# Two transformer-like blocks on one core: state matrices made earlier, the states' products in two portions, and another beginning of the program

## The reference

```python
# first stack, for layer in (0, 1)
h = h + token_mixer(rmsnorm(h), ...)     # a product with w_in gives v, q, k, u, gates; pooling; dilated attention
h = h + conv_ffn(rmsnorm(h), ...)        # a product of width 2 x 2816, a convolution over 3 tokens, gelu, gate, a product back
x = rmsnorm(h)
# second stack, layer 0: gated recurrence (hgrn2) beside a state-space layer (s5)
abar = exp(a * dt)                                 # complex, 32 groups x 64 states
s_t  = abar * s_{t-1} + bb @ u_t                   # "states"
y    = re(c @ s_t) + d * u_t ; z = gelu(y) ; z * sigmoid(z @ w_glu + b_glu)
h = h + concat(hgrn2, s5) @ w_out ; h = h + conv_ffn(...)
# layer 1: latent attention, conv_ffn, and a last rmsnorm
```

## Time and profile before

| | |
|---|---|
| median of 3 runs | 1554.23 us |
| the profiled execution | 1555.74 us |
| its span, first to last instruction | 1554.0 us |
| PE busy | 1497.6 us (96%) |
| DVE / ACT / POOL busy | 1098.1 / 769.0 / 471.2 us |
| mean clock granted to TensorE | 0.986 |

### The profile page before, as it was taken

One profiled execution on the slowest core, in us unless ns is written; L12 is line 12 of the kernel. 1 busy time (PEld: TensorE's weight loads), 2 busy tenths in 40 slices (PEclk: granted clock), 3 DMA queues, 4 the chain that ended last, 5 costly groups with the idle time before them and its releaser, 6 DMA issues.

```text
span 1554.0 us, 24766 instructions
## 1 busy us (share of the span) xinstructions
PE 1497.6 (96%) x10640; PEld 1364.8 (88%) x10640; DVE 1098.1 (71%) x1169; ACT 769.0 (49%) x869; POOL 471.2 (30%) x288
## 2 busy tenths in 40 slices
PE   6999999999999979999999999999999998899997
PEld 4899999888888978999888879898888898888886
DVE  6657666788767537666888555957987568688863
ACT  5433454666444323545656346346665444566542
POOL 1205300244209758001354813001444000135510
PEclk9999999999999989999999998899999999999999
DMA  6574344555554653366455443334554534355552
GB/s 248 196 217 173 134 180 175 188 190 190 176 198 174 252 205 121 136 247 228 183 190 183 152 157 133 110 109 163 190 190 177 186 131 138 109 170 186 188 189 81
DMA packets 48009, 269.72 MB, mean 174 GB/s; under 512 B 11259, under 2 KB 14587, under 8 KB 18716
## 3 DMA queue, kind: packets, MB, share of 16 engines
q1 hardware_dynamic: 47900, 268.13, 48.6%
HBM read 261.30 MB, written 6.82 MB: 173 GB/s over the span
## 4 chain that ended last, share of the span: by engine, by line
PE 85%; POOL 6%; DVE 4%; DMA 2%; ACT 2%; issue 1%; SPq 0%; DVEq 0%; ACTq 0%; POOLq 0%
PE gemm L564 32%; PE gemm L535 29%; PE aux L564 15%; POOL s_made L2041 2%; POOL s_cw L2041 2%; DVE w_lo L1361 2%; DMA raw<-in_weights 1%; POOL pool_w L2041 1%; ACT w_hi L1016 1%; PE aux L586 1%; PE gemm L955 1%; PE aux L535 1%; PE aux L760 1%; PE gemm L645 1%; DMA s_bc<-in_s_c 1%
## 5 line engine op out<-in xcount | busy, mean ns | idle before, releaser
L1361 DVE TENSOR_TENSOR w_lo<-raw,w_hi 128x2048 fp32r<-128x2048 f32 (+3 forms) x248 | 568.8, 2295 | 222.7 <-ACT w_hi L1016 219.7
L1016 ACT ACTIVATE w_hi<-raw 128x2048 fp32r<-128x2048 f32 (+3 forms) x248 | 460.7, 1858 | 359.5 <-PE gemm L535 204.7
L535 PE MATMUL gemm<-x_two,w_hi 128*128 128x256 f32 x1952 | 359.0, 286 | 0.0
L535 PEld LDWEIGHTS gemm<-x_two,w_hi 128*128 128x128 f32 x1952 | 307.8, 194 | 0.9 <-issue 0.2
L535 PE MATMUL gemm<-x_two,w_lo 128*128 128x256 f32 x976 | 277.8, 285 | 0.0
L564 PE MATMUL gemm<-x_two,w_hi 128*128 128x512 f32 x672 | 234.7, 399 | 0.0
L2041 POOL TENSOR_TENSOR tmp<-tmp 128x512 f32<-128x512 f32 x24 | 35.5, 1478 | 551.6 <-ACT tmp L1043 551.5
L535 PEld LDWEIGHTS gemm<-x_two,w_lo 128*128 128x128 f32 x976 | 188.9, 194 | 0.0
L564 PE MATMUL gemm<-y_two,w_hi 128*128 128x512 f32 x528 | 185.2, 396 | 0.0
L564 PE MATMUL gemm<-x_two,w_lo 128*128 128x256 f32 x672 | 174.9, 281 | 0.0
L2161 POOL TENSOR_TENSOR cv<-cv,rstd 128x512 f32<-128x512 f32 x44 | 117.0, 2659 | 174.6 <-ACT cv L1095 174.6
(11 more groups left out here) (364 smaller groups left out, 2726.4 us busy)
## 6 DMA issues: line engine op xcount, KB each, us to landing
raw<-in_weights SPq DMA_DIRECT2D x224, 1024.0 KB, 4.8
raw<-in_weights SPq DMA_DIRECT2D x16, 768.0 KB, 4.2
raw<-in_weights SPq DMA_DIRECT2D x4, 576.0 KB, 3.6
s_inputs<-s_made SPq DMA_DIRECT2D x1, 2048.0 KB, 7.3
s_outputs<-s_cw SPq DMA_DIRECT2D x1, 2048.0 KB, 7.3
s_v<-s_inputs SPq DMA_DIRECT2D x1, 2048.0 KB, 10.1
s_cw<-s_outputs SPq DMA_DIRECT2D x1, 2048.0 KB, 9.6
raw<-in_weights SPq DMA_DIRECT2D x4, 512.0 KB, 3.8
```

The source lines that it names most:

```text
L535: mm = pe.matmul(out, lhs, rhs, start=fresh and m == 0, stop=end and m == 2, skip_group_check=True)
L1016: me.give(act.activation(w_hi[i % SPL][:, 0:n], raw[i % RAW][:, 0:n], ACT.Copy), w_hi_ready)
L1361: me.give(v.tensor_tensor(w_lo[i % RAW][:, 0:n], raw[i % RAW][:, 0:n], w_hi[i % SPL][:, 0:n].bitcast(F32), ALU.subtract), w_lo_ready)
```

## The change

It has four parts.

1. **State matrices.** `s5_inputs` on POOL moves from behind layer 1's first norm sum to the gap behind the first network's last gate (before the norm sum). SP stores `s5_made` at v+1 instead of v+11, and `s5_cw` at v+15 instead of v+18. DVE waits for the second store before it writes gates over its source.
2. **Norm of the mixer.** In both mixers the sum of squares stands behind v1 instead of v0 on PE, the columns behind v2; ACT's root and DVE's reciprocal and v1's emptying move one block back with them.
3. **States' products.** `s5_from_states` is cut in two portions, one on each side of a block; ACT's gelu and DVE's low part of the result move behind other work. `s5_within` on DVE goes from one slot (4) to two (6 and 7).
4. **Program start.** x comes in four pieces, block 0 in two, the first 8 parameter columns alone and first; ACT and DVE work in that order; the squares come last of the inputs; ACT starts with a dummy copy; PE starts with 18 dummy products of a 128x128 tile of ones.

```diff
 # SP
-            load(h[:, :, :], a["x"].rearrange("(c p) s -> p c s", p=P), x_in)
-            load(par[:, :], a["params"], par_in)
+            load(par[:, 0:DC], a["params"][:, 0:DC], par0_in)
+            load_x(0)
+            load(raw[0][:, 0:HALF0], w0[:, 0:HALF0], raw0_in)
+            load_x(1)
+            load(raw[0][:, HALF0:WIDE], w0[:, HALF0:WIDE], raw_in[0])
+            load_x(2)
+            load_x(3)
...
-                if i == first("v", 1) + 11:
+                if i == first("v", 1) + 1:
                     sp.wait_ge(v_made, 1)
...
-                if i == first("v", 1) + 18:
+                if i == first("v", 1) + 15:
                     sp.wait_ge(cw_made, 1)
 # PE
+                if i == 0:
+                    parts = [range(0, 2), range(2, 4)]
...
-                    if j == 0:
...
+                    if j == 1:
                         norm(classes=True)
-                    if j == 1:
+                    if j == 2:
...
+            for k in range(WARM):
+                pe.matmul(A[:, 0:P], ones[:, :], ones[:, :], start=True, stop=True)
...
-            s5_from_states()
+            s5_from_states((0, 1))
             gemm(i + 8, x_hi, x_lo)
+            s5_from_states((2, 3))
             chunk_scores()
 # ACT (DVE alike)
+            first_feed(0)
+            act.wait_ge(raw0_in, 16)
+            me.give(act.activation(w_hi[0][:, 0:HALF0], raw[0][:, 0:HALF0], ACT.Copy), w0_hi_half)
+            first_feed(1)
+            act.wait_ge(raw_in[0], 16)
+            me.give(act.activation(w_hi[0][:, HALF0:WIDE], raw[0][:, HALF0:WIDE], ACT.Copy), w_hi_ready)
+            split(1)
+            first_feed(2)
+            first_feed(3)
+            for j in range(4):
+                me.give(act.activation(tmp[:, 2 * j:2 * j + 2, :], h[:, 2 * j:2 * j + 2, :], ACT.Square), pair_squared)
+            split(2)
 # DVE
             def s5_within(k):
-                if k != 4:
+                if k not in (6, 7):
                     return
...
-                for q in range(4):
+                for q in ((0, 1), (2, 3))[k - 6]:
...
+                if layer:
+                    v.wait_ge(cw_out, 16)
 # POOL
                     ffn(0)
+                    me.settle()
+                    s5_inputs()
                     sum_squares()
...
                 if layer:
-                    s5_inputs()
                     s5_outputs()
```

More of the change, by code:

```diff
@@ L38 @@
 SPL = 3
+HALF0 = WIDE // 2
+WARM = 18
 BANK = 512
@@ L432, in weights @@
                      a["weights"][OFFSETS[i] * P:OFFSETS[i + 1] * P].rearrange("(p n) -> p n", p=P), raw_in[i % RAW])
-            for i in range(RAW):
+            for i in range(1, RAW):
                 weights(i)
+                if i == 1:
+                    load(par[:, DC:NPAR], a["params"][:, DC:NPAR], par_in)
             load(relb[0:BUCKETS, :], a["rel_bias"], relb_in)
@@ L770, in s5_from_inputs, with s5_from_states @@
                                   start=g % 2 == 0 and d == 0, stop=False, skip_group_check=True)
-            def s5_from_states():
-                me.take(s_ready)
-                pe.wait_ge(cw_in, 16)
+            def s5_from_states(groups):
+                if 0 in groups:
+                    me.take(s_ready)
+                    pe.wait_ge(cw_in, 16)
                 m = None
-                for g in range(4):
+                for g in groups:
                     for c in range(T5):
@@ L1151, in mixer, with first_feed @@
                 feed_after(first("wo", layer), named(f"norm2.{layer}"))
-            act.wait_ge(par_in, 16)
[L1154 to L1160, removed]
+            me.take(ones_ready)
+            act.activation(small[:, 43:44], small[:, 0:1], ACT.Copy)
+            act.wait_ge(par0_in, 16)
+            def first_feed(j):
+                act.wait_ge(x_in[j], 16)
+                for c in (2 * j, 2 * j + 1):
+                    ins = act.activation(by_place(x_hi[:, c, :]), in_fours(h[:, c, :]), ACT.Copy, scale=vec("norm1.0", c))
+                me.give(ins, x_hi_ready)
+            first_feed(0)
[10 more added lines that the diff above has]
+            split(2)
+            act.wait_ge(par_in, 16)
             dt, mag = ang[3], ang[4]
@@ L1247, in _ @@
             split_next(i + 7)
+            split_next(i + 8)
+            act.wait_ge(h_ready, 1)
+            sigmoid_in(0)
+            me.take(ket_psum)
+            me.give(act.activation(ket.rearrange("p k n -> p (k n)"), A[:, 2 * BANK:4 * BANK], ACT.Copy), ket_ready)
             me.take(ys_ready)
@@ L1604, in _ @@
             me.give(v.memset(small[:, 1:4], 0.0), ones_ready)
-            v.wait_ge(par_in, 16)
[L1606 to L1612, removed]
+            v.wait_ge(par0_in, 16)
+            feed(0, named("norm1.0"), classes=True)
+            v.wait_ge(w0_hi_half, 1)
+            me.give(v.tensor_tensor(w_lo[0][:, 0:HALF0], raw[0][:, 0:HALF0], w_hi[0][:, 0:HALF0].bitcast(F32),
+                                    ALU.subtract), w0_lo_half)
+            feed(1, named("norm1.0"), classes=True)
+            v.wait_ge(w_hi_ready, 1)
+            me.give(v.tensor_tensor(w_lo[0][:, HALF0:WIDE], raw[0][:, HALF0:WIDE], w_hi[0][:, HALF0:WIDE].bitcast(F32),
+                                    ALU.subtract), w_lo_ready)
+            split(1)
+            feed(2, named("norm1.0"), classes=True)
+            feed(3, named("norm1.0"), classes=True)
+            split(2)
+            v.wait_ge(par_in, 16)
             theta, red = ang[5], ang[6]
```

51 lines of the change are left out of this document (31 added, 20 removed).

## The result

| | before | after |
|---|---|---|
| median | 1554.22 us (4 runs, 1549.85 to 1558.14) | 1527.81 us (4 runs, 1527.12 to 1528.96) |
| the profiled execution / its span | 1555.74 / 1554.0 us | 1528.17 / 1526.4 us |
| PE idle in the span | 56.4 us | 31.1 us |

What follows compares the result with a forecast made beforehand. PE bounds the kernel, busy 1497.6 of 1554.0 us. Terms 13.9 - 0.8 + 5.2 + 6.6 + 1.0 + 3.5 = 29.4 us take 1555.7 to 1526.3; the median lies 1.5 lower: 1525, range 1517 to 1534.

Steps and rivals of the forecast that it cites:

- matrices earlier: Layer 1's mixer: moving POOL's state matrices earlier removes PE's 12.2 us wait and 1.7 us of low clock: 13.9 us.
- norm one block later: Both mixers: PE waits 0.2 us, up to 1, at v4 for v1's bank; -0.8 us for both, bounds 0 and -2.
- DVE's slot: PE's wait at L738 for turned matrices goes, 3.6 us, and 1.6 us of low clock: 5.2 us.
- states in two portions: PE's instruction-fetch stop in the states' products goes, 3.8 us, and 2.8 us of low clock: 6.6 us, bounds 2 and 6.6.
- inputs' products: Stop behind product 157 of 256 goes because 18 dummies shift the instruction fetch: 1.0 us, low clock behind it not counted.
- program start: At the beginning v1 can start at 16.8 us, v2 at 25.8 against 29.2: 3.5 us, bounds 0 and 6.
- rival D: POOL's 24 operations at 3.6 us each block SP at v+2, decisive from about 3.5 each: 1564 us; chance 0.02.
- behind product 186 PE waits for its own instructions: In states' products PE stands 3.8 us for instructions; the 18 dummies move the place to 168, 40 products into the block.
- rival A: Clock stays up through the inputs' products: 4.9 us more gained, 1520 us; chance 0.17.
- rival C: The start gives nothing, since pieces of 1 KB rows and small parameters are slow: 1528.5 us; chance 0.06.
- block 1 has landed by 11.4: Program start: at 0.42 MB per us of DMA, block 1 lands at 11.4 us, so v1 can start at 16.8.
- S + 11.3 against S + 11.1: Mixers, S being v2's start: v1's bank is free at S + 11.3, PE wants v4 at S + 11.1; wait 0.2 us.

Runs made afterwards that it cites:

- run 5: The kernel after with the state matrices late again (POOL makes both behind the norm's sum, SP stores at v+11 and v+18): 1540.44 us.
- run 9: The kernel after with the columns' copy and v1's emptying ahead of v5's low part on DVE in both mixers: 1525.98 us.
- run 1: The kernel before with only the 18 dummy products added at PE's start: 1546.05 us against 1552.04.
- run 6: The kernel after with DVE's move of the within-chunk kernel in one piece in slot 4 again: 1531.86 us.
- run 2: The kernel after without the 18 dummy products: 1529.16 us.
- run 3: The kernel after with the states' products in one portion of 256 again, dummies kept: 1529.67 us.
- run 7: The kernel after with the old beginning (x in one load, all parameters, blocks 0 to 3 whole), dummies and later norm kept: 1527.0 us.
- run 4: The kernel after with the old beginning and 44 dummy products instead of 18: 1533.02 us.
- Run 8: The kernel after with block 1 loaded, copied, subtracted and used in halves too: 1530.06 us.
- 10: The kernel after with the old beginning, v1's emptying ahead of v5's low part, and the 18 dummies issued only when x has landed: 1525.59 us.
- 11: The kernel after with block 1 in halves and v1's emptying ahead of v5's low part: 1523.59 us.

## Why the prediction was right, and where it was wrong

By its own steps, in us of the profiled execution:

| step | forecast | trace | what the runs say |
|---|---|---|---|
| matrices earlier | 13.9 | 13.4 | run 5: 13.0 to 14.1 |
| norm one block later | -0.8 | -2.9 in layer 0, -1.3 in layer 1 | run 9 gives back 1.1 and 1.4; 1.7 of the 2.9 is clock that run 1 had too |
| DVE's slot | 5.2 | 5.2 | run 6: 4.9 |
| states in two portions | 6.6 | 6.3 | without dummies (run 2 against before) 6.3; with them (run 3) 2.0 |
| inputs' products | 1.0 | 6.0 | run 1: the whole 6.0; run 2: 2.6 |
| program start | 3.5 | 0.1 | run 7: 0.6 at v2 |
| latent attention, last network | none | +0.8 | clock, before and after; not tried |
| sum | 29.4 | 27.6 | |

The trace's 13.4 is the 12.1 gained in layer 1's mixer with the norm's 1.3 given back to it. The terms are not independent: the dummies and the portions each remove the states' stop. No run undoes the norm's move alone.

**Right with its mechanism.** SP's queue blocked by POOL, the cover of the loaded blocks, POOL's 45 us beside other neighbours, DVE's slot: place, size and witnesses came as written. The trace fits the rule weighed there from the Trainium skill (SBUF — State Buffer, section "Who interferes with whom"): the operations again took between 1.05 and 3.43 us, with the same sum. But rival D was placed too far off. By its own numbers (a start at 409.0, SP's wait from 452.8, 5.5 us of cover) PE would have waited from (458.3 - 409.0) / 24 = 2.05 us for each operation on, not from 3.5; they took 45.0 / 24 = 1.88.

**The fetch.** The step "behind product 186 PE waits for its own instructions" held in four runs, and the place moved with the dummies: 157, 186, 150 or 151, 197. The page on kernel launch (the Trainium skill, Runtime: NRT & Kernel Launch, section "Instruction fetch mechanics") would have it mostly hidden; runs 1 to 4 don't bear that out in bursts of products of 15 to 29 ns. What failed in the step is the count: 18 dummies move the grid by 36 products. The place in the new order was therefore 150, only 22 products into the block, 1.9 + 2.6 = 4.5 us behind the burst's start, not 6.7. By the forecast's own argument (there at 6.5) 2 us of the stop should have stayed. They didn't, so the argument about when a piece is asked for was wrong as well, and the two errors cancelled. A piece asked for some 165 products ahead of its place and there 5.4 to 6.6 us later is a fit to the eight stops seen (two before, the others in runs 1 to 4) and not more than that; the two of run 4 lie at its lower edge.

**The clock, rival A.** The 4.9 us behind the inputs' stop were put at 17%, and they came: without the stop there was no low clock in that stretch, in any run. So A's mechanism was the right one, and my reason against it (a stop of 1.0 us is short) was no reason. Nor did the small products bring the low clock: all 256 ran in 7.30 us at the whole one. The forecast's time was met without A only because other terms failed. But the step "a stop brings a low clock of 1.7 us" is not a law either. The stop of 0.68 us in run 2 brought 1.7, that of 1.94 in run 3 and that of 1.74 in run 1 brought nothing. Near 45 us a low clock stood in the kernel after and in runs 1, 2, 4, 6, 8 and 9, and in neither the kernel before nor runs 3, 5, 7, 10 and 11. The wait at the first table doesn't decide it: run 1 had none, and runs 3, 5 and 7 had the same 0.7 us as the kernel after. I can say what a low clock cost in a trace; I can't say what will bring it.

**The start, rival C's effect with another cause.** The failed step is "block 1 has landed by 11.4": I divided by the 0.42 MB per us of the earlier trace rows, which belongs to whole loads. In the new order the same stretch moved 0.6 MB less. And the low clock charged at 1.7 took 2.7 (half of 5.35 busy us from 17.8 to 24.6). Rival C named small pieces and small parameters; that fits the 0.6 MB, but the chain behind (copy, subtraction, pair of x) is longer than the DMA's share. Run 8 shows that: halves removed the 4 us with the DMA still slow.

**The norm.** "S + 11.3 against S + 11.1" was nearly right for what it counted, but v5's low part starts only when ACT's copy is there, and took 3.1 us in layer 1 (485.86) instead of 2.2, so the emptying ended at 490.5. That is 12.2 behind v2's start, 1.0 of wait. In layer 0 the bound was missed from another side: the first table stands ahead of v4 and needs the bank some 3.6 us before v4 does (it waited 0.7 us, to 41.4; v4 began at 45.0). The low clock from 45.1 to 48.5 behind it makes 1.7 of the 2.9 us, and since run 1 had one there with the norm in its old place, it is not shown to be the norm's. The loss of 4.2 in both layers is outside my bounds of 0 to -2. Run 9, without the two waits (1.7 us), gives back 2.5 of it by block 95, and half of that is lost again later.

So the forecast was 2.8 us off the median since an unforeseen 5 us of clock and 7 us of overestimates (start and norm) came nearly to the same, which is luck. Of the 2.8 us, 1.8 are in the sum (29.4 against 27.6). Most of the rest comes from the step to the median: the profiled execution lay 1.5 us above the median before and 0.4 above it after.

## What to carry to other kernels

A queue that waits for a slow producer is paid by whatever stands behind it in the queue: read that engine's own waits, subtract the cover of what is already loaded, and the gain of moving the store came out within half a us here. A stop without a releaser in the middle of a long run of tiny products was the instruction stream in this kernel. Look at which product it stands behind, add a few instructions ahead, and see whether the place moves. Then either put long work in the middle of the run or shift the place out of it, and count records in the trace, not calls in the code. Two cures of one stop don't add up: measure each with and without the other. A beginning is worth what its last input gains; find the load that the second block waits for, and see whether cutting the first ones in pieces delays it.

## What the runs showed of the hardware that I had not expected

- Places where PE ran out of instructions came 128 products (weight load and matmul) apart, and moved with the dummies ahead of them in the program, even 940 us earlier (with 18 dummies from 186 to 150 or 151; with 44 from 157 to 69, and the next place to 197, where PE stopped). A float32 dummy of 128x128 moved them by two.
- 18 dummy products at the start of the program changed the time by 0.3% (0.9954 to 0.9984), without any gain at the start.
- The granted clock reads 1.00 from 13.7 to 21.6 us in the kernel before, yet block 0's 24 products took 8.0 us there and 5.75 behind dummies. The first record of the clock in that trace is at 17.8 us: ahead of it the column says nothing.
- Single runs of the kernel before spread from 1546 to 1560 us, those of each kernel with fewer stops by 1.5 to 6 us, over far fewer runs. Whether the stops make the spread was not tried.
